# A two-layer hybrid decoder trunk on one core: cache copies, page loads and small attention steps in other places, and the compressed values by row groups

## What is computed

```python
def nsa_block(blk, kc, vc, kc_end, ksb, vsb, cover):
    ...
    p_c = masked_softmax(s_c, vis_c[None, :, None, None, :])
    o_c = jnp.einsum('bqgrc,bcgh->bqgrh', p_c.astype(vc.dtype), vc)
    ...
    o_s = jnp.einsum('bqgrk,bgqkh->bqgrh', p_s.astype(vs.dtype), vs)
    ...
    o_w = jnp.einsum('bqgrk,bkgh->bqgrh', p_w.astype(vw.dtype), vw)
    g = gates.reshape(bn, qb, N_KV, GROUP, 3)
    o = g[..., 0:1] * o_c + g[..., 1:2] * o_s + g[..., 2:3] * o_w

def trunk_layer(x, pos0, hist, w_in, ...):
    h = jnp.einsum('btd,de->bte', x, w_in)
    ...
    merged = (g_a * jnp.einsum('btc,cd->btd', y_a, proj_a)
              + g_b * jnp.einsum('btc,cd->btd', y_b, proj_b)
              + g_c * jnp.einsum('btc,cd->btd', y_c, proj_c))
    y = jnp.einsum('btd,de->bte', merged, w_out)
    out = layer_norm(ALPHA * x + y, ln_g, ln_b)
```

## Time and profile before

| | |
|---|---|
| median of 3 runs | 798.3 us (797.21 to 800.86) |
| the profiled execution | 795.67 us |
| its span | 794.0 us |
| granted TensorE clock, mean | 0.979 |
| busy: PE, DVE, ACT, POOL | 96%, 70%, 51%, 15% |
| HBM | 145.77 MB read, 13.34 MB written |

### The profile page before, as it was taken

One profiled execution on the slowest core, in us unless ns is written; L12 is line 12 of the kernel. 1 busy time (PEld: TensorE's weight loads), 2 busy tenths in 40 slices (PEclk: granted clock), 3 DMA queues, 4 the chain that ended last, 5 costly groups with the idle time before them and its releaser, 6 DMA issues.

```text
span 794.0 us, 16917 instructions
## 1 busy us (share of the span) xinstructions
PE 760.4 (96%) x6302; PEld 712.3 (90%) x6302; DVE 558.6 (70%) x996; ACT 408.1 (51%) x815; POOL 122.0 (15%) x210
## 2 busy tenths in 40 slices
PE   8999989999999889999999989899999899999994
PEld 8996888998899889999869989898888899999993
DVE  4474679998688376665774687899866686766675
ACT  5553367675556235444445455666654464444453
POOL 2431014310133100000600000343010000000033
PEclk9999999999999979999999999999999899999997
DMA  9987446633968955565627765465359555666631
GB/s 318 299 285 224 150 134 196 204 108 105 336 204 271 330 188 178 184 185 164 182 87 244 249 197 158 143 211 156 106 184 395 166 176 184 187 179 175 181 130 55
DMA packets 42619, 154.94 MB, mean 195 GB/s; under 512 B 6449, under 2 KB 7473, under 8 KB 41905
## 3 DMA queue, kind: packets, MB, share of 16 engines
q1 hardware_dynamic: 33952, 115.55, 46.5%
q0 software_dynamic: 8592, 38.37, 14.5%
HBM read 145.77 MB, written 13.34 MB: 200 GB/s over the span
## 4 chain that ended last, share of the span: by engine, by line
PE 84%; DMA 6%; DVE 5%; ACT 2%; issue 1%; SPq 0%; ACTq 0%; DVEq 0%
PE bank L713 22%; PE bank L714 22%; PE bank L715 21%; DMA ring<-weights_dram 6%; PE bank L731 3%; PE bank L932 3%; DVE w_lo L1274 1%; PE bank L876 1%; PE bank L882 1%; PE bank L912 1%; PE bank L887 1%; ACT probs L1184 1%; PE bank L924 1%; PE bank L914 1%; PE bank L913 1%
## 5 line engine op out<-in xcount | busy, mean ns | idle before, releaser
L1274 DVE TENSOR_TENSOR w_lo<-ring,w_hi 128x1024 fp32r<-128x1024 f32 x202 | 247.7, 1227 | 157.8 <-ACT w_hi L1075 154.2
L713 PE MATMUL bank<-x_hi,w_hi 128*128 128x264 f32 x1208 | 352.6, 292 | 1.3 <-DVE w_lo L1274 1.2
L715 PE MATMUL bank<-x_lo,w_hi 128*128 128x264 f32 x1208 | 344.1, 285 | 0.0
L714 PE MATMUL bank<-x_hi,w_lo 128*128 128x264 f32 x1208 | 344.1, 285 | 0.0
L1075 ACT ACTIVATE w_hi<-ring 128x1024 fp32r<-128x1024 f32 x202 | 213.5, 1058 | 74.7 <-DMA ring<-weights_dram 48.3
L713 PEld LDWEIGHTS bank<-x_hi,w_hi 128*128 128x128 f32 x1208 | 229.3, 190 | 5.6 <-issue 3.3
L714 PEld LDWEIGHTS bank<-x_hi,w_lo 128*128 128x128 f32 x1208 | 229.5, 190 | 0.6
L715 PEld LDWEIGHTS bank<-x_lo,w_hi 128*128 128x128 f32 x1208 | 228.3, 189 | 0.0
L713 PE MATMUL bank<-h_rounded,w_hi 128*128 128x264 f32 x352 | 101.7, 289 | 7.0 <-DVE w_lo L1274 6.8
L714 PE MATMUL bank<-h_rounded,w_lo 128*128 128x264 f32 x352 | 101.4, 288 | 0.0
L1127 ACT ACTIVATE h<-bank 128x264 f32<-128x264 f32 x88 | 34.7, 394 | 83.0 <-PE bank L715 78.0
(11 more groups left out here) (269 smaller groups left out, 1039.5 us busy)
## 6 DMA issues: line engine op xcount, KB each, us to landing
ring<-weights_dram SPq DMA_DIRECT2D x208, 512.0 KB, 3.8
cache_a<-kcmp_dram POOLq DMA_DIRECT2D x32, 128.0 KB, 3.9
cache_b<-vcmp_dram POOLq DMA_DIRECT2D x32, 128.0 KB, 3.7
cache_a<-ksel_dram POOLq DMA_DIRECT2D x32, 128.0 KB, 3.1
cache_b<-vsel_dram POOLq DMA_DIRECT2D x32, 128.0 KB, 3.2
cache_a<-kwin_dram POOLq DMA_DIRECT2D x2, 2048.0 KB, 11.6
cache_b<-vwin_dram POOLq DMA_DIRECT2D x2, 2048.0 KB, 8.5
kv_dram<-h POOLq DMA_DIRECT2D x2, 1056.0 KB, 6.1
```

The lines of the kernel that those rows point to most:

```text
L713: pe.matmul(out, w_high[:, k0 + k, :], high, start=(k == 0), stop=False)
L714: pe.matmul(out, w_rest[:, k0 + k, :], high, start=False, stop=False)
L715: ins = pe.matmul(out, w_high[:, k0 + k, :], rest, start=False, stop=(k == kn - 1))
L1274: dve.tensor_tensor(w_lo[:, slot % RING], ring[:, slot % RING], w_hi[:, d % HI_RING].bitcast(F32), ALU.subtract).then_inc(w_lo_ready, 1)
```

## The change

Six edits, all in the order and the placing of work.

- **Cache copies among the heads.** The two DRAM copies become four pieces each, issued by POOL behind the maxima of pairs 4, 5, 6 and 7 and ahead of the `kwin` load.
- **Pages in the merge.** The `kcmp` and `vcmp` loads for layer 1 also wait until DVE has emptied the first bank of `merge` 0.
- **First maxima ahead.** DVE's part of `cmp_soft` becomes the step `cmp_sums`, behind the first pair's maxima; `cmp_turn` follows the second `dense` tile of the heads instead of the first; `cs` moves from `probs` to the end of `m`.
- **Gates in two steps.** `gate_in` (DVE's `gate_d`) stays at tile 17 of the 25; `gates` (PE and the copies out of MI) goes to tile 18. In layer 1 `cmp_rope` goes from 17 to 18 with it.
- **Other last chain.** In the last layer two tiles are centered as soon as ACT has squared the mean, two more behind the variance; the last two tiles of the affine step go from ACT to DVE.
- **Compressed values of two pairs side by side.** The matmul L924 leaves `pv`. Two steps `cmp_pv` (pairs 1 and 2, after the odd `dense` tile) multiply only the 32 rows of each pair, two pairs per step in two row groups and two banks (PT0, PT1), both halves `gp` in one bank; ACT copies them to `cmp_o`. ACT's copy of `pv` becomes DVE's addition `pv_out` of bank OT and `cmp_o`, one in each pair.

```diff
-    {13: [("cmp_k", 0)], 14: [("cmp_v", 0)], 16: [("cmp_sum", 0)], 17: [("cmp_rope", 0)], 18: [("cmp_sum", 1)]})
+    {13: [("cmp_k", 0)], 14: [("cmp_v", 0)], 16: [("cmp_sum", 0)], 18: [("cmp_rope", 0), ("cmp_sum", 1)]})
...
-    15: [("rope", 3)], 17: [("gates", 0), ("rope", 4)], 18: [("k_split", 0)], 19: [("rope", 5)], 
+    15: [("rope", 3)], 17: [("gate_in", 0), ("rope", 4)], 18: [("gates", 0), ("k_split", 0)], 19: [("rope", 5)], 
...
         order.append(("scores", p))
+        if p == 0:
+            order.append(("cmp_sums", 0))
...
-            if u == 0:
+            if u == 1:
                 order.append(("cmp_turn", 0))
...
+            if u in CMP_PV_AFTER:
+                order.append(("cmp_pv", CMP_PV_AFTER.index(u)))
             if g2 and p > 0:
                 order.append(("pv", p - 1))
             if g2:
                 order.append(("scale", u))
+            if g2 and p > 0:
+                order.append(("pv_out", p - 1))
...
+CMP_PV_AFTER = (3, 5)
 GATE_RING = 3
+COPIES = 4
...
+                for n in range(COPIES):
+                    pool.wait_ge(max_ready, l * HEADS + HEADS - 2 * (COPIES - n) + 2)
+                    go()
+                    rows = slice(n * P // COPIES, (n + 1) * P // COPIES)
+                    pool.dma_start(kwin_out[l, rows], kwin[l, rows]).then_inc(win_copied, 16)
+                    pool.dma_start(vwin_out[l, rows], vwin[l, rows]).then_inc(win_copied, 16)
+
                 wait_filled(pool, l, "one_scores", 0)
...
                     wait_filled(pool, l, "one_scores", 1)
+                    wait_emptied(pool, l, "merge", 0)
                     go()
                     load_pages(l + 1, kcmp, cmp_dst(cmp_view[0]), cmp_k_landed)
...
-                pool.dma_start(kwin_out[l], kwin[l]).then_inc(win_copied, 16)
-                pool.dma_start(vwin_out[l], vwin[l]).then_inc(win_copied, 16)
...
+                    elif step == "cmp_pv":
+                        wait_emptied(pe, l, "cmp_turn", 0)
+                        wait_emptied(pe, l, "cmp_vrows", 0)
+                        outs = [out_bank(step, i, j) for j in range(2)]
+                        for gp in range(GP):
+                            for j in range(2):
+                                r = 2 * i + j
+                                rows = slice(32 * r, 32 * r + 32)
+                                ins = pe.matmul(outs[j][:, gp * SEQ:(gp + 1) * SEQ], vc_bd[rows, gp, r, :],
+                                                pc_t[rows, gp, :], start=(gp == 0), stop=(gp == GP - 1),
+                                                skip_group_check=True)
...
-                        pe.matmul(out[:, 0:SEQ], vc_bd[:, gp, r, :], pc_t[:, gp, :], start=True, stop=False,
-                                  skip_group_check=True)
...
-                    elif step == "pv":
-                        wait_filled(act, l, step, i)
-                        emptied_by(act.activation(h[:, Q + i, 0:SEQ], bank[OT][:, 0:SEQ], ACT.Copy), step, i)
+                    elif step == "cmp_pv":
+                        act.wait_ge(k_stored, (l + 1) * 16)
+                        for j in range(2):
+                            wait_filled(act, l, step, i, j)
+                            emptied_by(act.activation(cmp_o[i][j], bank[(PT0, PT1)[j]][:, :].rearrange(
+                                "p (g t) -> p g t", g=GP), ACT.Copy), step, i, j)
...
+                    elif step == "pv_out":
+                        gp, r = i // R, i % R
+                        wait_filled(dve, l, "pv", i)
+                        wait_emptied(dve, l, "cmp_pv", r // 2, r % 2)
+                        emptied_by(dve.tensor_tensor(h[:, Q + i, 0:SEQ], bank[OT][:, 0:SEQ], cmp_o[r // 2][r % 2][:, gp, :],
+                                                     ALU.add), "pv", i)
...
+                        if l == DEPTH - 1:
+                            dve.wait_ge(mean_squared, l + 1)
+                            center(0, 2)
...
+                            for n in (KT8 - 2, KT8 - 1):
+                                ins = dve.tensor_scalar(m[:, n, :], z[:, n, :], pr("ln_g", n, 1), pr("ln_b", n, 1),
+                                                        ALU.mult, ALU.add)
+                            ins.then_inc(last_ready, 1)
```

More of the change, by code:

```diff
@@ L139, in make_order @@
     order += [("turn", HEADS - 2), ("one_cmp_scores", 0), ("one_scores", 0), ("dense", 41), ("turn", HEADS - 1),
-              ("dense", 42), ("pv", PAIRS - 1), ("one_turn", 0), ("conv", 0), ("dense", 43), ("one_pv", 0), ("conv", 1),
+              ("dense", 42), ("pv", PAIRS - 1), ("pv_out", PAIRS - 1), ("one_turn", 0), ("conv", 0), ("dense", 43), ("one_pv", 0), ("conv", 1),
               ("dense", 44), ("conv", 2), ("dense", 45), ("one_scores", 1), ("dense", 46), ("one_turn", 1),
@@ L203, in banks_of @@
         return [(KEPT + 3 * KT8 + i) % 2]
-    if step == "turn":
+    if step in ("turn", "cmp_pv"):
         return [PT0, PT1]
@@ L275 @@
 ROPE_Z = [0, 2, 0, 2, 4, 6]
-VECTOR_STEPS = 102
+VECTOR_STEPS = 100
 def trunk(nc, x_in, weights, params, consts, pages, kcmp, vcmp, ksel, vsel, kwin, vwin,
@@ L369, in trunk @@
         hc_ext = mf[:, 0:4 * (2 + SEQ)].rearrange("p (g t) -> p g t", g=4)
+        cmp_o = [[flat[:, at + j * GP * SEQ:at + (j + 1) * GP * SEQ].rearrange("p (g t) -> p g t", g=GP)
+                  for j in range(2)] for flat, at in ((hk, 0), (mf, KT8 * T - 2 * GP * SEQ))]
         g = h[:, CC:CC + 3 * GATE_RING, :].rearrange("p (a j) t -> p a j t", j=3)
         probs_flat = probs[:, :, :].rearrange("p a n -> p (a n)")
-        cs = probs_flat[:, 768:768 + 32 * CT].rearrange("p (n c) -> p n c", c=CT)
+        cs = mf[:, KT8 * T - 32 * CT:KT8 * T].rearrange("p (n c) -> p n c", c=CT)
         cs_t = probs_flat[:, 0:GP * SEQ]
@@ L932, in _ @@
                                     ins = pe.matmul(out[g2 * HD:g2 * HD + HD, q0:SEQ], v_rows[:, half, col:col + HD],
-                                                    probs_t[:, g2, br, k0:k0 + SEQ - q0], start=False,
-                                                    stop=(br == 1 and half == 1), skip_group_check=True)
+                                                    probs_t[:, g2, br, k0:k0 + SEQ - q0],
+                                                    start=(br == 0 and half == 0), stop=(br == 1 and half == 1), skip_group_check=True)
                         done(ins, step, i)
@@ L1256, in _ @@
                         round_next(step, i)
-                        for n in range(KT8):
+                        for n in range(KT8 - 2 if l == DEPTH - 1 else KT8):
                             if n % 2 == 0:
@@ L1316, in _ @@
                                                      ALU.mult), step, i)
-                    if step == "gates":
+                    if step == "gate_in":
                         wait_emptied(dve, l, "dense", NG)
@@ L1443, in _ @@
                                           z_r[:, Q_HI + i % 2, 0:SEQ].bitcast(F32), ALU.subtract).then_inc(q_split, 1)
-                    elif step == "cmp_soft":
+                    elif step == "cmp_sums":
                         dve.wait_ge(cmp_exped, l + 1)
@@ L1684, in _, with center @@
                     elif step == "norm":
+                        def center(first, n):
+                            part = z[:, first:first + n, :]
+                            dve.tensor_tensor(part, part, bank[SA][:, 0:T].unsqueeze(1).to_broadcast([P, n, T]),
+                                              ALU.subtract).then_inc(centered, 1)
+                        if l == DEPTH - 1:
+                            dve.wait_ge(mean_squared, l + 1)
+                            center(0, 2)
                         dve.wait_ge(mean_squared, l + 1)
@@ L1688, in _ @@
                         dve.wait_ge(var_ready, l + 1)
-                        def center(first):
-                            part = z[:, first:first + 4, :]
-                            link(dve.tensor_tensor(part, part, bank[SA][:, 0:T].unsqueeze(1).to_broadcast([P, 4, T]),
-                                                   ALU.subtract))
-                        center(0)
+                        if l == DEPTH - 1:
+                            center(2, 2)
+                        else:
+                            center(0, 4)
+                        dve.wait_ge(centered, 2 * l + (2 if l == DEPTH - 1 else 1))
                         dve.wait_ge(std_ready, l + 1)
@@ L1701, in _ @@
                             if k == 2:
-                                center(4)
+                                center(4, 4)
+                                dve.wait_ge(centered, 2 * l + (3 if l == DEPTH - 1 else 2))
                             if l == DEPTH - 1:
```

15 lines of the change are left out of this document (10 added, 5 removed).

## The result

| | before | changed |
|---|---|---|
| median of 4 runs each | 797.9 us (797.21 to 800.86) | 772.22 us (770.73 to 772.43) |
| the profiled execution, its span | 795.67, 794.0 us | 772.43, 770.6 us |
| granted TensorE clock, mean | 0.979 | 0.996 |

The ratio is 0.9692, 95% interval 0.9668 to 0.9715: faster. Forecast were 772.6 us, range 766.5 to 780.0. One execution of the run "Only the pages as before" took 3978.53 us; it counts in that run's median alone.

What follows compares the result with a forecast made beforehand. TensorE (PE) was taken as the bound, through its idle and lower-clock time; 15.4 + 6.9 + 1.3 + 0.8 + 1.2 = 25.6 us off 795.67 gave 770.1, times 1.0033 = 772.6 us, range 766.5 to 780.0.

Steps and rivals of the forecast that it cites:

- Cache copies and pages, 15.4: Merge and layer 1: moving the copies removes two PE stalls and the half clock behind them, 9.5 + 5.9 us.
- Zero for the pages: Merge: pages loaded beside weights cost nothing, with up to 5 us if the first weight is held.
- "Nothing" for the cover among the heads: Heads: five slots hold some 27 us of work, so copy pieces cost nothing; without cover, 16 us a layer.
- First maxima, 6.9: Heads' start: earlier maxima save PE's 2.6 us wait in layer 0 and 2.6 + 1.7 in layer 1.
- 1.7 (the 0.61 stretch): Heads' start, layer 1: 4.40 us busy at granted clock 0.61 costs 39%, 1.7 us, counted as gained.
- Values, 1.3: Heads: compressed values in row groups gain net 0.67 us a layer (-3.44 + 1.72 + 0.3 + 0.75), 1.3 in both.
- I take 0.75: Heads: time per layer that comes back as PE waits for DVE's `probs_t`, between 0 and 3.2 us.
- the slower rival: Heads: DVE becomes the bound through `pv_out`; 52 us go, 822 us; chance 0.03.
- Gates, 0.8: Gates, layer 1: a wait of some 2.2 us replaces 2.15; gain 0.8, between nothing and 3.7.
- Last chain, 1.2: Kernel's end: earlier centering about 0.6 us, plus affine tiles shared with DVE; together 1.2, between 0.5 and 1.7.
- The rivals: Weights held up elsewhere 0.10; row groups give nothing 0.08; gates' edit works 0.06; DVE bounds heads 0.03; copies not the holder 0.02.

Runs made afterwards that it cites:

- Only the pages as before: The changed kernel with only the pages' wait for the merge removed, the copies staying among the heads; 772.86 us, ratio 0.9683.

## Why the prediction was right

*The sum.* 25.6 us were forecast against the profiled execution; 23.4 of span came, and 25.7 between the medians. That the time hit to 0.4 us owes something to luck in the scaling: I put the result 0.33% above the profiled level, as the median of before stood, while the changed kernel's profiled execution lies 0.2 us above its own median. On the profiled level the forecast was 770.1 and the time 772.43.

*Cache copies and pages, 15.4.* Right in cause and size: 16.1 by the undoing. Zero for the pages is right as well. "Nothing" for the cover among the heads is right with a bound: in one piece the copies cost 1.3.

*First maxima, 6.9.* 6.84 by the undoing. Between the two traces the heads give 3.12 + 3.29 = 6.41, the values' edit with them. Held against the run with the old values, whose stretches from the masks to the first `pv` are 16.48 and 16.68, the kernel before lost 3.03 in layer 0 and 3.84 in layer 1, together 6.87: the sum is right, but its parts, 2.6 and 4.3, are not, and that they cancel is luck. The step that failed is "1.7 (the 0.61 stretch)" as a fixed price of layer 1: in the kernel before, layer 1 took only 20.52 - 19.51 = 1.0 longer than layer 0, where no clock fell, and the run with the maxima undone lost the clock in layer 0 instead. One reason is seen in the traces: layer 0 without the fall had a wait of 0.3 for `probs_t` that layer 1 with it had not. Half of a stretch at lower clock is its price only where no other wait lies in it.

*Values, 1.3.* The mechanism was right, the size off: 0.44 in the heads, 0.15 over the span. The groups do run side by side, and with their switches cost 2.12 where I had 1.72 + 0.3 = 2.02. (The row that I read as two matmuls shows the two records of one; its 0.43 is the price of one, as I used it.) The Trainium skill ("TensorEngine Tiling (Array Packing)", Tiling Modes, Key Properties) says that a change of the tiling mode drains TensorE. This trace leaves little room for that: 2.12 less 1.72 is 0.4 a layer, 0.2 for each `cmp_pv`. The step that failed is "I take 0.75" given back: it was 1.1 a layer, so that almost all the gain went. DVE did not become the bound of every pair, as the slower rival has it, nor was it 97% busy: over the seven pairs of layer 0 the windows' sum has 70.27 of 75.20 us, 93%.

```profile
sum 75.20, PE 74.26 PEld 67.19 DVE 70.27 ACT 51.14 POOL 26.39; mean PE 10.61 PEld 9.60 DVE 10.04 ACT 7.31 POOL 3.77
```

The four waits for `probs_t` that went with the pooling steps' move are those behind pairs in which such a step stood between `pv_out` and the next maxima.

*Gates, 0.8.* The wait was forecast as 2.2 and is 1.98. The clock behind it did not fall in the profiled execution, so 2.1 came there; with the fall it is 0.9.

*Last chain, 1.2.* 0.7: half-size centerings cost 0.70, not 0.6, and two affine tiles on DVE take 0.74 of the 1.05 back (0.42 + 0.3 came).

*The rivals.* None came true: no weight in the changed kernel lands later than 8.9 us, the row groups run in couples, PE still waits 1.98 at the gates and for `probs_t` 0.6 at most at a time, and the copies did hold the tile.

## What to carry to other kernels

A long transfer is cheap where the buffers ahead of the bound engine hold more work than it lasts: the same 16 us of held weight cost PE a wait of 6.8 us at the merge, and the clock behind it, and waits of 0.5 to 0.9 among the heads. Work taken off the bound engine and given to a neighbour that is 93% busy counts in full only where the neighbour's own order has room (here 0.44 of 2.64, and 1.70 with other steps of the neighbour moved); look at what stands between the added step and the next thing the bound engine waits for. Twice here a wait whose step was put one place later came back at another user; it went when the work of the late engine was spread.

## What the runs showed that I had not expected

The fall of TensorE's clock behind a gap is not a property of the kernel. Eight profiled executions, of eight kernels, have the gates of the changed kernel, with PE idle 1.96 to 3.14 us there. In six the granted clock then fell, to between 0.50 and 0.76 in the following windows of 3 us; in two (waits of 1.98 and 1.96) it stayed at 1.00, and one of the six had a wait of 1.98 as well. Two rows behind nearly equal waits (1.98 and 1.96), of the run with the copies in one piece and of the one with the old values:

```profile
459.00:462.00 3.00, 2.35 (x8) 2.06 (x9) 2.71 (x6) 1.01 (x2) 0.00 (x0) 0.61 0.35 135
```

```profile
459.00:462.00 3.00, 3.00 (x27) 3.00 (x26) 2.78 (x11) 0.37 (x2) 0.00 (x0) 1.00 0.05 19
```

What decides is not shown; the run with one piece had another wait of 1.1 some 11 us earlier. By the mean clocks one kernel goes either way, too: the four executions of the run with one piece have mean clocks of 0.993 and 0.994 (spans 773.7 and 773.1) and twice 0.996 (770.7 and 771.0), while all four of the changed kernel have 0.996. The fall is worth about 1.2 us (283.94 against 282.71). So a gap of 2 us has a price of its own and one that comes only in some executions, and a difference of 1 us between the spans of two single profiles says nothing about an edit; stretches away from such a gap say more.
